# A gated state-space and retention block on one core: left operands of two matrix products split straight from SBUF, half of the squares folded by VectorE, S5's constants computed in pieces

## The chip, the cores and the metric

The kernel runs on one core of a Trainium2 chip (trn2). The metric is the device time of one execution in microseconds (us), and the figure for a kernel is the median of its runs. TensorE does the matrix products, ScalarE and VectorE prepare their operands and take the results, GpSimd and SyncE mostly issue transfers.

## The reference

Input x is 1024 tokens by 2048 channels in float32. One layer is computed:

```
h = RMSNorm_pre(x);  P = h @ W_in      # columns: u, s5 gate, q, k, v, ret gate, two merge gates
y_s = S5(u) -> GELU -> half-GLU, times SiLU(s5 gate)
y_r = retention(q, k, v) -> per-head RMSNorm, times SiLU(ret gate)
m = sigmoid(g_s) * (y_s @ W_s) + sigmoid(g_r) * (y_r @ W_r)
x = x + RMSNorm_post(m @ W_out)
```

S5 is a diagonal complex recurrence. Its constants come from `lam_re`, `lam_im` and `log_step` (64 groups by 64 states): `step = exp(log_step)`, `mag = exp(lr * step)`, the cosine and sine of `li * step`, their powers up to the eighth, and a factor that scales B.

## The kernel before

**Matrix products.** All of them are cut into 16 output groups, in this order: u, v, zr, zs, gs0, gs1, qk, glu, gr0, gr1, ws0, ws1, wr0, wr1, out0, out1 (`GU`, `GV`, ... `GO1`). Each group is a 2 by 2 block product by a Strassen-Winograd scheme with seven products, p = A11, S1, S2, S4, S3, A12, A22 in order of time, and each product is 8 steps (4 in glu and ws0 to wr1), one for each tile of 128 in the inner dimension. That makes 756 steps. `at` is the number of a step in its group, 0 to 55. S1 = A21 + A22, S2 = S1 - A11, S4 = A12 - S2, S3 = A11 - A21 are sums of blocks of the left operand; the right operand's sums are made by `weights_summed`, one tile ahead by three steps.

**One step.** The products have nearly float32 precision: both 128x512 operands are split into a rounded part and the rest. ScalarE makes `a_hi` and `b_hi` (`heads`, L643 and L653), VectorE makes `a_lo` and `b_lo` (`rests`, L1085 and L1087), and TensorE does 12 matmuls of 512 columns (`multiply`, L1469 to L1475): four output tiles by hi*hi, hi*lo, lo*hi. The four rings have `RING = 3` slots, so that ScalarE can start step s only when step s-3 is done. Every engine has one program, a loop over the steps, and works in its written order: on VectorE a step is `weights_summed(s + 3)`, `rests(s)`, then evacuations (`evacuate`, 128x2048) and whatever else has been given to this step.

**Left operands.** They go through HBM. The blocks and their sums are written to `aops` (`store_ops`, 1 MB in each of two transfers) and read back a tile of 256 KB at a time into the 4 slots of `araw` (`load_a`, SyncE's queue). This holds for h in group u and for m in group out0 too, which stand whole in SBUF (`h_t`, `m_t`) while their first group runs. There each product's stores stand in SyncE's queue just ahead of its first load, which waits for them: at u's step 0 A11, at 8 S1, and so on; in out0 A12, A22 and S3 are stored at step 12. The sums are made by `left_sums`: in u and out0, at steps 5 and 6 S1, 7 and 8 S3 (in place over A21), 11 and 12 S2, 18 and 19 S4, each a 128x2048 operation. S2 overwrites S1's buffer, and S4 that of S2, so each waits for the store of the one before.

**Start.** x comes transposed in eight transfers of 1 MB (`load_x`) on SyncE's queue, four of them ahead of the first weights. ScalarE squares each (128x2048, L629), TensorE adds over partitions with a matrix of ones (L1437, four float32 matmuls for each, which the profile records as eight), ScalarE takes the root (L633, L635), VectorE the reciprocal (L1048) and scales h (`scale_h`, L1052, 128x512). The squares have a ring of two. VectorE first computes two exponentials (`magnitudes`). It scales half 0 of the tokens (16 operations) ahead of step 0, half 1 at steps 1 to 4, four each.

**S5's constants.** In group v VectorE computes `angles` (step 2), `quadrants` (4), `powers` (6) and `factors` (8), all chains of 128x64 operations each of which waits for the last; then `inputs_scaled` (9 to 16, 128x1024) and 24 `window_part`s (20 to 43), and in zr 24 `m3_part`s (4 to 27), one in a step. TensorE takes the windows after v's last step and the scan's inputs after zr's. In out0 and out1 `take_rows` scales results into `o_row`, which lies over `m_t`; `merge` (wr1 and the first steps of out0) completes m.

**ScalarE as a queue.** ScalarE also issues the stores of the results: u's go out in 16 transfers with short rows (L727), four at steps 37, 45 and 53 of u and 5 of v.

Of the kernel before, what the change touches and what calls it, by code (L numbers as in the profile page):

```python
# [90 lines left out]

def sums_before(g, p, k):

    order = {1: 0, 2: 1, 4: 2, 6: 3}
    return 4 * sum(TILES[:g]) + order[p] * TILES[g] + k
# [7 lines left out]
def build_program(nc, x, xT, wstream, gain_in, gain_out, b_glu, lam_re, lam_im, log_step,  # L103
                  b_ri, b_ir, c_ri, c_ir, d_rep, signs, eye, ones, dmat, zeta, xi,
                  gdec, rope, aops, spill, vrows, turned, m1d, m2d, m3d, out):
    with ExitStack() as ctx:
# [51 lines left out]
        powers_tmp = area(14336, 1024).rearrange("p (n g) -> p n g", n=16)  # L158
# [48 lines left out]
        rstd = keep[:, 2, 0:1024].rearrange("p (i n) -> p i n", i=2)  # L207
# [4 lines left out]
        squared, sums_done = sem("squared"), sem("sums_done")  # L212
# [60 lines left out]
        def token_as_step(a):  # L273
            return a.rearrange("p n (c t) -> p n t c", t=STEP)

# [34 lines left out]
        def _(sp):  # L310
# [31 lines left out]
            def store_ops(g, p):  # L342

                last = g == GO0
                for n in range(2):
                    ks = slice(4 * n, 4 * n + 4)
                    src = h_t if not last else m_t
                    if p in (A11, A12, A22):
                        i, first = (1, 8) if p == A22 else (0, 8 if p == A12 else 0)
                        if not last:  # L350
                            sp.wait_ge(h_ready, 16 * i + first + 4 * n + 4)
                        else:
                            sp.wait_ge(gated, {A11: 11, A12: 15, A22: 16}[p])
                        sp.dma_start(op_block(OP_BASE[g] + 8 * p + 4 * n), src[:, i, first + 4 * n:first + 4 * n + 4, :]
                                     ).then_inc(op_stored[p], 16)
                    else:
                        order = {S1: 0, S3: 1, S2: 2, S4: 3}[p]
                        sp.wait_ge(s_ready, (8 if last else 0) + 2 * order + n + 1)
                        if p == S3:
                            src = src[:, 1, ks, :]  # L360
                        elif last:
                            src = s_out(n).rearrange("p (k m) -> p k m", k=4)
                        else:
                            src = s_buf[:, ks, :]
                        sp.dma_start(op_block(OP_BASE[g] + 8 * p + 4 * n), src).then_inc(op_stored[p], 16)

            def load_a(s):
# [4 lines left out]
                if g in (GU, GO0):  # L372
                    sp.wait_ge(op_stored[p], 64 if g == GO0 else 32)
# [60 lines left out]
            for k in range(4):  # L434
                load_b11(0, k)
            for q in range(4, 8):
                load_x(q)
            for k in range(4, 8):
                load_b11(0, k)
            for s in range(STEPS):  # L440
                g, p, k = place(s)
                at = s - BASE[g]
                if g == GU and k == 0:
                    store_ops(g, p)
                if g == GO0 and k == 0 and p < 4:
                    store_ops(g, p)
                if g == GO0 and at == 12:
                    for later in (A12, A22, S3):
                        store_ops(g, later)
                load_a(s)  # L450
                if s >= A_RING:
# [3 lines left out]
                    if p4 == 6 and g4 + 1 < len(TILES):  # L455
                        load_b11(g4 + 1, k4)
# [79 lines left out]
                if g == GO0 and at == 36:  # L536
                    for p2 in (S1, S2, S4):
                        sp.wait_ge(op_stored[p2], 64)
                    sp.dma_start(gain_row, gain_out).then_inc(gain_row_loaded, 16)
# [17 lines left out]
        def _(pool):  # L557
# [4 lines left out]
            for p in range(7):  # L562
                pool.wait_ge(op_stored[p], 32)
            for dst, src in ((bb_p, b_ri), (bb_q, b_ir), (cc_p, c_ri), (cc_q, c_ir)):
                pool.dma_start(dst.rearrange("p g h -> p (g h)"), src).then_inc(params_loaded, 16)
# [52 lines left out]
        def _(act):  # L618
# [4 lines left out]
            act.wait_ge(eps_ready, 1)  # L623
            for q in range(8):
# [6 lines left out]
                if q == 4:  # L631
                    act.wait_ge(sums_done, 4)
                    A.activation(rstd[:, 0, :], psum[:, 4, :], ACT.Sqrt, scale=1.0 / D_MODEL, bias=eps_sb[:, 0:1]).then_inc(std_ready, 1)  # L633
            act.wait_ge(sums_done, 8)
            A.activation(rstd[:, 1, :], psum[:, 5, :], ACT.Sqrt, scale=1.0 / D_MODEL, bias=eps_sb[:, 0:1]).then_inc(std_ready, 1)  # L635

            def heads(s):
                g, p, k = place(s)
                r = s % RING
                act.wait_ge(a_loaded[s % A_RING], 16 * (s // A_RING + 1))  # L640
# [14 lines left out]
            def free(b, g):  # L655

                if g == 0:
                    act.wait_ge(sums_done, 8)
                    act.wait_ge(h_ready, 32)
# [157 lines left out]
            for s in range(STEPS + TAIL):  # L817
                if s < STEPS:
                    heads(s)
                over = ended(s - 3)  # L820
# [30 lines left out]
        def _(dve):  # L851
# [41 lines left out]
            def magnitudes():  # L893
                dve.wait_ge(rates_loaded, 5 * 16)
                exp(s0, step_sb, s1, s2, s3)
# [4 lines left out]
            def angles():  # L900
# [8 lines left out]
                then(V.scalar_tensor_tensor(s1, s3, -4.0, s1, ALU.mult, ALU.add))  # L909
                tt(s5, s2, s2, ALU.mult)  # L910
                poly(s6, s5, [2.7557319e-6, -1.98412698e-4, 8.33333333e-3, -1.66666667e-1, 1.0])
                tt(s6, s6, s2, ALU.mult)
                poly(s7, s5, [2.48015873e-5, -1.38888889e-3, 4.16666667e-2, -0.5, 1.0])

            def quadrants():
# [9 lines left out]
                tt(s7, s7, s6, ALU.add)  # L925
                ts(s3, s1, 2.0, ALU.is_ge, -2.0, ALU.mult)
# [8 lines left out]
            def powers():  # L935
# [4 lines left out]
                for m in (1, 2, 4):  # L940
                    re_m = pow_re[:, m:m + 1, :].broadcast_to([P, m, GROUPS])
                    im_m = pow_im[:, m:m + 1, :].broadcast_to([P, m, GROUPS])
                    p_rr, p_ii, p_ri, p_ir = [powers_tmp[:, 4 * n:4 * n + m, :] for n in range(4)]
                    V.tensor_tensor(p_rr, pow_re[:, 1:1 + m, :], re_m, ALU.mult).then_inc(setup_step, 1)
                    V.tensor_tensor(p_ii, pow_im[:, 1:1 + m, :], im_m, ALU.mult).then_inc(setup_step, 1)
                    V.tensor_tensor(p_ri, pow_re[:, 1:1 + m, :], im_m, ALU.mult).then_inc(setup_step, 1)
                    V.tensor_tensor(p_ir, pow_im[:, 1:1 + m, :], re_m, ALU.mult).then_inc(setup_step, 1)
                    steps[0] += 4
                    dve.wait_ge(setup_step, steps[0])
                    V.tensor_tensor(pow_re[:, m + 1:2 * m + 1, :], p_rr, p_ii, ALU.subtract).then_inc(setup_step, 1)  # L950
                    steps[0] += 1
                    tt(pow_im[:, m + 1:2 * m + 1, :], p_ri, p_ir, ALU.add)

            def factors():
# [3 lines left out]
                then(V.reciprocal(s1, s1))  # L958
# [8 lines left out]
                tt(par_im, s2, s1, ALU.mult)  # L967
                for par in range(2):
# [74 lines left out]
            magnitudes()  # L1043
            dve.wait_ge(consts_loaded, 5 * 16)

# [8 lines left out]

            invert(0)
            for k in range(16):
# [23 lines left out]
            def rests(s):  # L1080
# [4 lines left out]
                V.tensor_tensor(a_lo[:, r, :], araw[:, s % A_RING, :], a_hi[:, r, :].bitcast(F32), ALU.subtract).then_inc(split, 1)  # L1085
# [11 lines left out]
            def left_sums(g, a, at):  # L1097

                last = g == GO0
                for n in range(2):  # L1100
                    ks = slice(4 * n, 4 * n + 4)
                    k2 = slice(8 + 4 * n, 12 + 4 * n)
                    s_n = s_out(n).rearrange("p (k m) -> p k m", k=4) if last else s_buf[:, ks, :]
                    done = 8 if last else 0
                    stores = 64 if last else 32
                    if at == 5 + n:
                        if last:
                            dve.wait_ge(gated, 16)
                        else:
                            dve.wait_ge(h_ready, 32)  # L1110
                        V.tensor_tensor(s_n, a[:, 1, ks, :], a[:, 1, k2, :], ALU.add).then_inc(s_ready, 1)
                    if at == 7 + n:
                        dve.wait_ge(s_ready, done + n + 1)
                        V.tensor_tensor(a[:, 1, ks, :], a[:, 0, ks, :], a[:, 1, ks, :], ALU.subtract).then_inc(s_ready, 1)
                    if at == 11 + n:
                        dve.wait_ge(op_stored[S1], stores)
                        V.tensor_tensor(s_n, s_n, a[:, 0, ks, :], ALU.subtract).then_inc(s_ready, 1)
                    if at == 18 + n:
                        dve.wait_ge(op_stored[S2], stores)
                        V.tensor_tensor(s_n, a[:, 0, k2, :], s_n, ALU.subtract).then_inc(s_ready, 1)  # L1120
# [163 lines left out]
            def take_rows(g, p):  # L1284
# [7 lines left out]
                if g == GO0 and p == 3:  # L1292
                    dve.wait_ge(gain_row_loaded, 16)
                    for op in range(7):
# [414 lines left out]
```

## Time and profile before

| | us |
|---|---|
| median of 3 runs | 2518.59 |
| lowest and highest | 2516.74, 2531.87 |
| profiled execution: time | 2524.69 |
| profiled execution: span | 2522.9 |

The profile is of one execution. Its span is 1.8 us shorter than its time; the execution is 6.1 us above the median. Busy shares in it are averages over stages with different limits, so that the steps of the prediction go by stretches of time.

### The profile page before, as it was taken

What the parts mean: (1) busy time and instruction counts of PE and PEld (TensorE: products, weight loads), DVE (VectorE), ACT (ScalarE), POOL (GpSimd) and SP (SyncE); (2) the same over time, 40 slices, a digit from 0 to 9 for tenths busy, and PEclk for the clock granted to TensorE, in tenths of its full rate; (3) what the DMA queues carried; (4) which work ended last, traced back from release to release, by engine and by line L of the source; (5) the groups of instructions that cost most, each with busy time, mean ns of one, the idle gap of its engine ahead of it and who ended that gap; (6) DMA issues with size and microseconds to landing.
All of it is one profiled execution on the core that took longest, in us unless ns stands there. A gap on an engine that the chain in (4) does not pass through costs nothing.

```text
span 2522.9 us, 28579 instructions
## 1 busy us (share of the span) xinstructions
PE 2332.7 (92%) x10288; PEld 1892.8 (75%) x10288; DVE 1853.4 (73%) x2968; ACT 1150.8 (46%) x1814; POOL 85.2 (3%) x99
## 2 busy tenths in 40 slices
PE   7898999998999999988989996989999999799994
PEld 3676778787888888886777774767887777578883
DVE  6857992977898886626887754777678988767676
ACT  4343443456555554553445443334555444245552
POOL 0000000000000000000000000440000000000000
PEclk9999997999999999999999997899999999999997
DMA  7678456765456473769555767255656655855546
GB/s 271 217 232 253 133 171 217 262 209 197 120 183 211 145 244 111 256 199 296 180 184 157 280 187 255 68 201 175 212 196 210 224 185 180 291 200 189 182 130 254
DMA packets 287888, 508.67 MB, mean 202 GB/s; under 512 B 53201, under 2 KB 69601, under 8 KB 285569
## 3 DMA queue, kind: packets, MB, share of 16 engines
q1 hardware_dynamic: 242672, 430.00, 52.1%
q10 hardware_dynamic: 36560, 46.27, 5.3%
q0 software_dynamic: 8512, 30.56, 3.7%
q8 instruction: 81, 1.33, 0.2%
q14 instruction: 63, 0.51, 0.1%
HBM read 394.54 MB, written 112.20 MB: 201 GB/s over the span
## 4 chain that ended last, share of the span: by engine, by line
PE 67%; DVE 16%; DMA 6%; issue 4%; ACT 3%; SPq 3%; ACTq 1%; POOL 0%; DVEq 0%; POOLq 0%
PE psum L1473 16%; PE psum L1474 16%; PE psum L1475 16%; PE psum L1469 4%; PE psum L1471 4%; PE psum L1470 4%; DMA araw<-aops 4%; DVE a_lo L1085 3%; DVE b_lo L1087 3%; PE psum L1580 1%; PE psum L1578 1%; ACT a_hi L643 1%; DVE keep L1095 1%; PE psum L1529 1%; DMA aops<-work 1%
## 5 line engine op out<-in xcount | busy, mean ns | idle before, releaser
L643 ACT ACTIVATE a_hi<-araw 128x512 fp32r<-128x512 f32 x756 | 476.5, 630 | 1197.5 <-PE psum L1475 760.8
L1473 PE MATMUL psum<-a_hi,b_hi 128*128 128x512 f32 x2352 | 930.9, 396 | 97.8 <-DVE b_lo L1087 90.7
L1474 PE MATMUL psum<-a_hi,b_lo 128*128 128x512 f32 x2352 | 923.7, 393 | 0.0
L1475 PE MATMUL psum<-a_lo,b_hi 128*128 128x512 f32 x2352 | 922.8, 392 | 0.0
L1085 DVE TENSOR_TENSOR a_lo<-araw,a_hi 128x512 fp32r<-128x512 f32 x756 | 520.9, 689 | 535.5 <-ACT a_hi L643 534.1
L1473 PEld LDWEIGHTS psum<-a_hi,b_hi 128*128 128x128 f32 x2352 | 446.6, 190 | 213.5 <-DVE b_lo L1087 107.7
L1475 PEld LDWEIGHTS psum<-a_lo,b_hi 128*128 128x128 f32 x2352 | 446.5, 190 | 94.5
L1474 PEld LDWEIGHTS psum<-a_hi,b_lo 128*128 128x128 f32 x2352 | 446.8, 190 | 91.6
L1469 PE MATMUL psum<-b_hi,a_hi 128*128 128x512 f32 x672 | 268.4, 399 | 30.2 <-DVE b_lo L1087 29.6
L1087 DVE TENSOR_TENSOR b_lo<-bx,b_hi 128x512 fp32r<-128x512 f32 x432 | 295.5, 684 | 0.0
L653 ACT ACTIVATE b_hi<-bx 128x512 fp32r<-128x512 f32 x432 | 266.5, 617 | 0.5 <-DMA bx<-in_wstream 0.2
L1470 PE MATMUL psum<-b_lo,a_hi 128*128 128x512 f32 x672 | 265.6, 395 | 0.0
L1471 PE MATMUL psum<-b_hi,a_lo 128*128 128x512 f32 x672 | 265.1, 394 | 0.0
L1469 PEld LDWEIGHTS psum<-b_hi,a_hi 128*128 128x128 f32 x672 | 128.5, 191 | 66.6 <-DVE b_lo L1087 34.8
L1471 PEld LDWEIGHTS psum<-b_hi,a_lo 128*128 128x128 f32 x672 | 128.6, 191 | 27.4
L1470 PEld LDWEIGHTS psum<-b_lo,a_hi 128*128 128x128 f32 x672 | 128.7, 191 | 26.4
L1087 DVE TENSOR_TENSOR b_lo<-bz,b_hi 128x512 fp32r<-128x512 f32 x216 | 147.8, 684 | 0.0
L653 ACT ACTIVATE b_hi<-bz 128x512 fp32r<-128x512 f32 x216 | 133.2, 617 | 0.0
L692 ACT ACTIVATE keep<-psum 128x2048 f32<-128x2048 f32 x63 | 117.4, 1863 | 7.0 <-PE psum L1471 6.9
L1095 DVE TENSOR_TENSOR keep<-psum,keep 128x2048 f32<-128x2048 f32 x48 | 109.6, 2283 | 0.0
L1067 DVE TENSOR_TENSOR bx<-by,bx 128x512 f32<-128x512 f32 x108 | 74.1, 686 | 2.0
L1071 DVE TENSOR_TENSOR bx<-bz,bx 128x512 f32<-128x512 f32 x108 | 73.9, 684 | 1.8
(147 smaller groups left out, 1618.8 us busy)
## 6 DMA issues: line engine op xcount, KB each, us to landing
araw<-aops SPq DMA_DIRECT2D x744, 256.0 KB, 2.7
bz<-in_wstream SPq DMA_DIRECT2D x216, 256.0 KB, 3.7
bx<-in_wstream SPq DMA_DIRECT2D x116, 256.0 KB, 4.7
aops<-work SPq DMA_DIRECT2D x28, 1024.0 KB, 5.7
spill<-keep ACTq DMA_DIRECT2D x28, 1024.0 KB, 5.8
by<-in_wstream SPq DMA_DIRECT2D x108, 256.0 KB, 5.5
work<-spill SPq DMA_DIRECT2D x20, 1024.0 KB, 7.6
aops<-work POOLq DMA_DIRECT2D x15, 1024.0 KB, 5.4
```

The lines of the kernel that those rows point to most:

```text
L643: A.activation(a_hi[:, r, :], araw[:, s % A_RING, :], ACT.Copy).then_inc(head, 1)
L653: A.activation(b_hi[:, r, :], src[:, k, :], ACT.Copy).then_inc(head, 1)
L692: A.activation(kept_view(g, b), bank_view(g, banks), func).then_inc(act_evac, 1)
L1085: V.tensor_tensor(a_lo[:, r, :], araw[:, s % A_RING, :], a_hi[:, r, :].bitcast(F32), ALU.subtract).then_inc(split, 1)
L1087: V.tensor_tensor(b_lo[:, r, :], src[:, k, :], b_hi[:, r, :].bitcast(F32), ALU.subtract).then_inc(split, 1)
L1095: V.tensor_tensor(kept_view(g, b), bank_view(g, banks), kept_view(g, b), ALU.add).then_inc(dve_evac, 1)
L1469: T.matmul(bank, a_hi[:, r, cols], b_hi[:, r, :], start=first, stop=False, skip_group_check=on)
L1470: T.matmul(bank, a_hi[:, r, cols], b_lo[:, r, :], start=False, stop=False, skip_group_check=on)
L1471: done = T.matmul(bank, a_lo[:, r, cols], b_hi[:, r, :], start=False, stop=last, skip_group_check=on)
L1473: T.matmul(bank, b_hi[:, r, cols], a_hi[:, r, :], start=first, stop=False, skip_group_check=on)
L1474: T.matmul(bank, b_lo[:, r, cols], a_hi[:, r, :], start=False, stop=False, skip_group_check=on)
L1475: done = T.matmul(bank, b_hi[:, r, cols], a_lo[:, r, :], start=False, stop=last, skip_group_check=on)
```

## The change

- **Left operands in u and out0.** The new function `left(s)` gives the tile of `h_t`, `s_buf`, `m_t` or `s_out`, and `heads` and `rests` read it there. `load_a` isn't called in these groups. ScalarE waits for VectorE's semaphores (`h_ready`, `s_ready`, `gated`) in place of a load's. The stores of the blocks stay, for the later groups, at steps 16 (S1), 18 (A11), 20 (A22), 24 (S2), 32 (S4), 36 (A12), 40 (S3) of SyncE's program. The first group that reads them back is v, or out1.
- **Sums.** In u they are made a tile at a time (`sum_h`, 128x512): S1 at steps 4 to 11, together with the scaling of the two tiles of half 1 that it needs, S2 at 14 to 21, S4 at 22 to 29 together with the scaling of A12's tile, S3 at 30 to 37. Ahead of step 0 stand only 8 of the 16 scalings. The second reciprocal stands at step 3. In out0 (`sum_m`, 128x2048): S1 at 5 and 6, S2 at 14 and 18, S4 at 22 and 26, S3 at 28 and 30.
- **Squares.** For half 0 VectorE adds the four tiles of each square (`fold`), and TensorE does one matmul in place of four. Half 1 stays with TensorE; its last two squares are summed between steps 0 and 1 and between 1 and 2. x and the first weights are loaded alternately. A root of one column ahead of the squares loads ScalarE's table.
- **Constants.** One exponential stays at the start, ahead of the folds. The rest goes to u's steps 38 (`magnitudes`), 42, 44, 46, 48, 50, 52, 54 and v's 0, 2, 4, 6. `inputs_scaled` moves to 8 to 15, `window_part` to two of three steps in 17 to 52, `m3_part` in zr to two of three steps in 4 to 39.
- **Rows out.** out0's four `take_rows` move to out1's steps 1 to 4.

```
+            if p == A11:
+                return whole[:, 0, k, :]
...
             for s in range(STEPS):
...
+                if g in (GU, GO0):
+                    if at == 16:
+                        store_ops(g, S1)
...
+                else:
+                    load_a(s)
...
-                A.activation(a_hi[:, r, :], araw[:, s % A_RING, :], ACT.Copy).then_inc(head, 1)
+                A.activation(a_hi[:, r, :], left(s), ACT.Copy).then_inc(head, 1)
...
+            def fold(q):
+
+                dve.wait_ge(squared, q + 1)
+                V.tensor_tensor(sq_ring[:, q % 2, 0:1024], sq_ring[:, q % 2, 0:1024], sq_ring[:, q % 2, 1024:2048], ALU.add
+                                ).then_inc(folded, 1)
+                dve.wait_ge(folded, 2 * q + 1)
+                V.tensor_tensor(sq_ring[:, q % 2, 0:512], sq_ring[:, q % 2, 0:512], sq_ring[:, q % 2, 512:1024], ALU.add
+                                ).then_inc(folded, 1)
...
             invert(0)
-            for k in range(16):
+            for k in range(8):
                 scale_h(0, k)
...
+            def sum_h(p, k):
+
+                a11, a12, a21, a22 = h_t[:, 0, k, :], h_t[:, 0, 8 + k, :], h_t[:, 1, k, :], h_t[:, 1, 8 + k, :]
+                if p == S1:
+                    dve.wait_ge(h_ready, h_order(1, 8 + k) + 1)
+                    V.tensor_tensor(s_buf[:, k, :], a21, a22, ALU.add).then_inc(s_ready, 1)
+                elif p == S2:
+                    dve.wait_ge(s_kept[k // 4], 16)
+                    V.tensor_tensor(s_buf[:, k, :], s_buf[:, k, :], a11, ALU.subtract).then_inc(s_ready, 1)
...
                 if g == GU:
+                    if at == 3:
+                        invert(1)
+                    if 4 <= at < 12:
+                        scale_h(1, at - 4)
+                        scale_h(1, at + 4)
+                        sum_h(S1, at - 4)
+                    if 14 <= at < 22:
+                        sum_h(S2, at - 14)
+                    if 22 <= at < 30:
+                        scale_h(0, at - 14)
+                        sum_h(S4, at - 22)
+                    if 30 <= at < 38:
+                        sum_h(S3, at - 30)
+                    if at == 38:
+                        magnitudes()
+                    if at == 42:
+                        quarter_turns()
...
+                if s in (0, 1):
+                    sum_squares(6 + s)
```

## Rows read from the trace of the kernel before

**Rows 1.** The profile's page: busy time by engine

```profile
PE 2332.7 (92%) x10288; PEld 1892.8 (75%) x10288; DVE 1853.4 (73%) x2968; ACT 1150.8 (46%) x1814; POOL 85.2 (3%) x99
```

**Rows 2.** Busy time by stretch: length, then each engine's (instructions), granted clock, DMA

```profile
45.65:95.40 49.75, 39.66 (x144) 30.15 (x145) 46.56 (x56) 16.14 (x27) 0.00 (x0) 0.89 0.60 206
95.40:221.85 126.45, 122.07 (x530) 100.05 (x529) 81.85 (x119) 53.67 (x90) 2.12 (x4) 0.99 0.76 248
221.85:390.15 168.30, 157.38 (x661) 124.57 (x660) 152.47 (x267) 70.17 (x114) 4.79 (x7) 0.98 0.56 171
426.70:587.00 160.30, 155.92 (x661) 126.42 (x662) 121.42 (x169) 73.61 (x115) 9.92 (x16) 0.97 0.73 239
764.20:916.50 152.30, 152.30 (x674) 126.11 (x673) 132.60 (x372) 77.71 (x120) 0.00 (x0) 1.00 0.56 180
2154.45:2239.90 85.45, 66.17 (x254) 51.89 (x253) 60.91 (x71) 29.28 (x45) 0.00 (x0) 0.88 0.78 283
```

**Rows 3.** The chain of waits, 0 to 82 us: start, length, what

```profile
9.93 16.96 PE psum L1437 x32
27.74 3.36 DVE keep L1048
31.13 5.40 DVE work L1052 x8
36.55 4.42 DMA aops<-work
40.98 2.66 DMA araw<-aops
...
54.07 2.66 DVE work L1052 x4
```

**Rows 4.** The timeline, 0 to 28 us: start, length, engine, what, idle before

```profile
15.21 0.34 PEld L1437 LDWEIGHTS psum<-keep,ones_sb 128*128 128x128 f32 x1 [0.52 <-issue]
...
16.41 0.19 PEld L1437 LDWEIGHTS psum<-keep,ones_sb 128*128 128x128 f32 x1 [0.24 <-issue]
16.42 0.48 DVE L867 TENSOR_TENSOR work<-work 128x64 f32<-128x64 f32 x2
16.67 1.91 ACT L629 ACTIVATE keep<-work 128x2048 f32<-128x2048 f32 x1 [4.56 <-PE psum L1437]
...
22.22 0.48 DVE L867 TENSOR_TENSOR work<-work 128x64 f32<-128x64 f32 x2
```

**Rows 5.** VectorE's timeline in u: a right and a left operand's sum

```profile
64.35 0.69 DVE L1067 TENSOR_TENSOR bx<-by,bx 128x512 f32<-128x512 f32 x1
...
66.16 2.28 DVE L1111 TENSOR_TENSOR work<-work 128x2048 f32<-128x2048 f32 x1
```

**Rows 6.** ScalarE's timeline in u: its issues of u's stores

```profile
160.47 6.67 ACTq L727 DMA_DIRECT2D turned<-keep  x2
...
186.81 5.59 ACTq L727 DMA_DIRECT2D turned<-keep  x2
...
209.59 3.16 ACTq L727 DMA_DIRECT2D turned<-keep  x2
```

**Rows 7.** VectorE's timeline in v: first and last of `angles`, one of `inputs_scaled`

```profile
223.98 0.65 DVE L862 TENSOR_SCALAR work<-work 128x64 f32<-128x64 f32 x3
...
230.33 0.20 DVE L862 TENSOR_SCALAR work<-work 128x64 f32<-128x64 f32 x1
...
260.87 1.22 DVE L867 TENSOR_TENSOR work<-work 128x1024 f32<-128x1024 f32 x1
```

**Rows 8.** ScalarE's timeline in out0: the a_hi with the longest waits ahead

```profile
2187.22 0.63 ACT L643 ACTIVATE a_hi<-araw 128x512 fp32r<-128x512 f32 x1 [15.36 <-DMA araw<-aops]
...
2209.80 0.63 ACT L643 ACTIVATE a_hi<-araw 128x512 fp32r<-128x512 f32 x1 [14.64 <-DMA araw<-aops]
```

**Rows 9.** VectorE's timeline at out0's start: the merges that complete m

```profile
2151.90 2.28 DVE L1279 TENSOR_TENSOR work<-work,keep 128x2048 f32<-128x2048 f32 x1
...
2154.22 2.29 DVE L1282 TENSOR_TENSOR work<-work 128x2048 f32<-128x2048 f32 x1
```

More of the change, by code:

```diff
@@ L274, in token_as_step, with left @@
             return a.rearrange("p n (c t) -> p n t c", t=STEP)
+        def left(s):
+            g, p, k = place(s)
+            if g not in (GU, GO0):
+                return araw[:, s % A_RING, :]
+            whole = m_t if g == GO0 else h_t
+            if p == A11:
+                return whole[:, 0, k, :]
+            if p == A12:
+                return whole[:, 0, 8 + k, :]
+            if p == A22:
+                return whole[:, 1, 8 + k, :]
+            if p == S3:
+                return whole[:, 1, k, :]
+            return s_out(k // 4)[:, COLS * (k % 4):COLS * (k % 4) + COLS] if g == GO0 else s_buf[:, k, :]
         def main_banks(g):
@@ L442, in _ @@
                 at = s - BASE[g]
[L443 to L450, printed above, removed]
+                if g in (GU, GO0):
+                    if at == 16:
+                        store_ops(g, S1)
+                    if at == 18:
+                        store_ops(g, A11)
+                    if at == 20:
+                        store_ops(g, A22)
+                    if at == 24:
+                        store_ops(g, S2)
+                    if at == 32:
+                        store_ops(g, S4)
+                    if at == 36:
+                        store_ops(g, A12)
+                    if at == 40:
+                        store_ops(g, S3)
+                else:
+                    load_a(s)
                 if s >= A_RING:
@@ L560, in _ @@
                 pool.dma_start(dst, src).then_inc(consts_loaded, 16)
-            for p in range(7):
+            for p in (A11, S4, S3, A12, A22):
                 pool.wait_ge(op_stored[p], 32)
+            pool.wait_ge(split, 2 * BASE[GV])
             for dst, src in ((bb_p, b_ri), (bb_q, b_ir), (cc_p, c_ri), (cc_q, c_ir)):
@@ L621, in _, with square @@
                 act.dma_start(dst, src).then_inc(rates_loaded, 16)
-            act.wait_ge(eps_ready, 1)
-            for q in range(8):
+            def square(q):
                 act.wait_ge(x_loaded[q], 16)
@@ L630, in _, with root @@
                              ).then_inc(squared, 1)
[L631 to L635, printed above, removed]
+            def root(i):
+                act.wait_ge(sums_done, 4 * i + 4)
+                A.activation(rstd[:, i, :], psum[:, 4 + i, :], ACT.Sqrt, scale=1.0 / D_MODEL, bias=eps_sb[:, 0:1]).then_inc(std_ready, 1)
+            act.wait_ge(eps_ready, 1)
+            A.activation(rstd[:, 1, 0:1], eps_sb[:, 0:1], ACT.Sqrt)
+            for q in range(4):
+                square(q)
+            root(0)
+            square(4)
+            square(5)
             def heads(s):
@@ L819, in _ @@
                     heads(s)
+                if s == 0:
+                    square(6)
+                if s == 1:
+                    square(7)
+                if s == 2:
+                    root(1)
                 over = ended(s - 3)
@@ L957, in factors @@
                 tt(s1, s1, s2, ALU.add)
-                then(V.reciprocal(s1, s1))
+                V.reciprocal(s1, s1).then_inc(powers_ready, 1)
+                dve.wait_ge(powers_ready, 1)
+            def factors():
                 ts(s0, pow_re[:, 1, :], -1.0, ALU.add)
@@ L967, in factors, with scan_factors @@
                 tt(par_im, s2, s1, ALU.mult)
+            def scan_factors():
                 for par in range(2):
@@ L1053, in scale_h @@
                                        ALU.mult, ALU.mult).then_inc(h_ready, 1)
+            for q in range(4):
+                fold(q)
             invert(0)
-            for k in range(16):
+            for k in range(8):
                 scale_h(0, k)
@@ L1084, in rests @@
                 dve.wait_ge(head, 2 * s + 1)
-                V.tensor_tensor(a_lo[:, r, :], araw[:, s % A_RING, :], a_hi[:, r, :].bitcast(F32), ALU.subtract).then_inc(split, 1)
+                V.tensor_tensor(a_lo[:, r, :], left(s), a_hi[:, r, :].bitcast(F32), ALU.subtract).then_inc(split, 1)
                 dve.wait_ge(head, 2 * s + 2)
@@ L1293, in take_rows @@
                     dve.wait_ge(gain_row_loaded, 16)
-                    for op in range(7):
+                    for op in (A11, S4, S3, A12, A22):
                         dve.wait_ge(op_stored[op], 64)
@@ L1368, in _ @@
+                if g == GV:
+                    if at == 0:
+                        more_powers(4)
                     if at == 2:
-                        angles()
+                        inverse_rates()
                     if at == 4:
-                        quadrants()
+                        factors()
                     if at == 6:
-                        for op in range(7):
-                            dve.wait_ge(op_stored[op], 32)
-                        powers()
-                    if at == 8:
-                        factors()
```

248 lines of the change are left out of this document (149 added, 99 removed).

## The prediction

> **What bounds the kernel now.** The page comes first: TensorE is busy 92% of the span [rows 1]. That number doesn't say what a change at an edge is worth, so the second view is busy time by stretch, cut at starts of steps. The undisturbed middle sets the unit: group gs0 takes 152.3 us for 56 steps [rows 2], 2.72 us a step, with TensorE never idle. Each other stretch is held against that. u's steps 0 to 11 take 49.75 us for 12 x 2.72 = 32.6, so 17.1 are lost; u's other 44 steps lose 126.45 - 119.7 = 6.8; v's first 55 lose 168.3 - 149.6 = 18.7; zr's first 55 lose 10.7; out0's first 21 lose 85.45 - 57.1 = 28.3. Ahead of all that lies the start, 45.7 us until the first step. The third view, the chain of waits [rows 3], shows what the start is made of: sums on TensorE, a reciprocal, eight scalings, then 4.4 us for a store to land and 2.7 us for a load of the same data. The fourth, the timelines of ScalarE and VectorE, tells whose the losses are: in out0 ScalarE sits idle 15.4 and 14.6 us until a load of `araw` [rows 8], in v VectorE works on its small operations for 6.5 us at a stretch [rows 7]. A step needs some 1.2 us of splitting on VectorE (four scalings of 2.66 us with it made a period of 3.85 in u [rows 3]) and 0.6 for a right operand's sum, if several follow closely. So it has about 0.9 us a step to give away.
>
> The slack matters below. ScalarE may split step s when s-3 is done, and the halves are ready some 1.9 us after that (a_hi, b_hi, then b_lo), 3.5 us ahead of need. One delay of up to 3.5 us on VectorE costs nothing.
>
> **The start, to step 12.** Removed: the store and load in front of step 0 (4.42 + 2.66) [rows 3]. Added: the folds, behind one exponential. That exponential ends at 16.66, halfway in the first row of the pair [rows 4]; TensorE began its sums at 9.93 [rows 3], so the folds start later than the sums did. A fold is a 128x1024 and a 128x512 operation, 1.22 [rows 7] and 0.69 [rows 5], with a wait 1.95. Its matmul is two of the eight records of a square; they stood 0.86 apart (0.34 + 0.52) until about 16 us and 0.43 apart (0.19 + 0.24) after it [rows 4], so the one now takes about 1.7 at the lower of the clock's two levels (1.2 GHz). With a ring of two the third square (1.91) waits for the first sum: 16.7 + 1.95 + 1.7 = 20.4, square to 22.4, the fourth to 24.4, fold to 26.4, sum to 28.1, root 28.9, reciprocal (3.36) to 32.4, eight scalings (5.4) to 37.8, first split to 39.1. The sums of half 0 end 1.2 us later than the 26.89 of before; nothing is gained there. TensorE meanwhile has squares 4 and 5 to sum, 16 records from 30.9: seven at the lower level (6.0) and nine at 0.43, to 40.8. It is the later of the two, so step 0 starts at 40.8, not 45.7. The two moved sums (8 x 0.43 = 3.4 each) then lie on TensorE between steps 0 to 2: 53.1. ScalarE's root of half 1 waits for them, `heads(3)` is queued behind it, VectorE splits step 3 by 55.8, and its reciprocal (3.36) holds up the split of step 4, which TensorE starts at 60.5. Steps 4 to 11 each add two scalings and a sum, 2 x 0.67 + 0.65, to 0.6 and 1.2: 3.8 us a step, bound by VectorE. Step 12 starts at 60.5 + 30.4 = 90.9, against 95.4: **4.5 us gained**. The bounds: all of the 16 records at the lower level (13.7) take 3.9 off; none there adds 1.7, as the splits are ready at 39.1. So 0.6 to 6.2.
>
> Here the trace speaks first on a second point: a 128x2048 sum took 2.28, a 128x512 one 0.69 [rows 5]. The Trainium skill, "VectorE: DVE Perf Modes", section on the TRN2 errata, says that SBUF-source operations pay a fixed latency for each instruction, so that many small tiles pay it each, and this speaks against sums by tiles. The rows agree: 4 x 0.69 is 0.48 more than 2.28, in 8 replaced operations 3.8 us of VectorE's time. Operations that follow each other closely start 0.60 apart, which would leave 1.6.
>
> **u from step 12.** S2's sums make a step 0.6 + 0.6 + 1.2 = 2.4, S4's with a scaling 2.5, S3's 2.4: under 2.72, nothing lost, but hardly any slack is rebuilt. ScalarE waits for these sums two steps ahead of need. S2 and S4 overwrite what is being stored, but the stores of 1 MB have at least three steps (8 us) for the 4.4 of [rows 3]; SyncE's queue has no loads waiting behind them up to step 36, where loads of weights come that have four steps to spare. Lost before were 6.8, nearly all where ScalarE was held by the issue of u's stores: the second pairs of issues took 6.7 and 5.6 us at steps 37 and 45, against 3.2 at 53, which cost nothing [rows 6]. These stay. With less traffic about (56 loads are gone) they may shrink; I take no gain. New is the chain of small operations: `magnitudes` 6.0 (16.66 to 22.70 in [rows 4]), the former `angles` 6.5 for 27 operations [rows 7], 0.24 each, so 4.4 for the 18 of the quadrants and some 3.4 for those of the powers. In steps 38 to 55 VectorE gets 18 x 1.2 + 8 x 0.6 + two evacuations of 2.2 + 20.3 = 51.1 us for 49.0 of TensorE. That is 2.1 over. And `magnitudes` comes right after the issue at step 37, when all slack is used: 6.0 + 1.2 against 2.72 loses up to 4.5. Between 0 (the issues shrink and slack absorbs it) and 9 (both, with the lower clock behind the gap) I take **5 lost**.
>
> **v and zr.** Gone from v's first 16 steps are 20 us of small operations, what is left (powers of m = 4, the reciprocal, `factors`, the copies) is about 7.5 in 8 steps: 8 x 1.2 + 3 x 0.6 + 7.5 = 18.9 under 21.8. `inputs_scaled` makes 0.6 + 1.2 + 1.22 = 3.05 a step, 0.33 over, 2.6 in eight steps, within the slack. The window parts at two in three steps average 0.8 and fit. Of 18.7 lost I leave 1.7 (a late load at step 21 and an evacuation): **17 gained**, 13 to 18. ScalarE's evacuation of u's last product now waits for VectorE at v's step 2, with 1.3 us to spare. In zr the m3 parts' excess goes: **1.5 gained**, 0 to 2; the other 9 lie with a low clock after the windows and a late load at step 20, which stay.
>
> **out0 and out1.** No step waits for a store or a load of m now. What is late next is VectorE: two merges of 4.5 [rows 9] at steps 0 and 4 and two sums of 2.2 at 5 and 6. Run by hand from step 0 at 2154.5: step 1 0.7 late, steps 5, 6 and 7 0.2, 1.4 and 1.4 late, and from then on sums 4 steps apart fit. **28.3 becomes 3.2, 25 gained**, 20 to 27. The weights' loads are no longer queued behind A11's store. In out1 four `take_rows` of 2.2 follow each other with 1.2 each: 0.7 over a step, 2.8, within the slack; **0.5 lost**, 0 to 3.
>
> **The sum.** 4.5 - 5 + 17 + 1.5 + 25 - 0.5 = 42.5. The profiled execution's 2524.7 becomes 2482.2. It lies 6.1 above the median of the runs; from the median, 2518.6 - 42.5 = 2476.1. All terms at their lower ends give 0.6 - 9 + 13 + 0 + 20 - 3 = 21.6, 2497; at the upper 6.2 + 0 + 18 + 2 + 27 - 0 = 53.2, 2465.
>
> **Rivals.** (1) The queue of ScalarE lets go: with u's loads away the issues at 37 and 45 take 4 us like the later ones and cost nothing, and u from 12 gains 4.7 (6.8 less the 2.1 over) where I have 5 lost. Against it, S3's store stands at the same place as A12's did. Net 52, 2467. Start 0.6, u 9 lost, the rest as forecast: net 34.6, with v's at its low end 30.6, 2488. (3) A store takes the loads' place in out0: SyncE's stores of S1 wait behind A22's and the weights', and VectorE, which waits for S1's landing at step 14, holds all splits. Before, such landings cost 14.6 us of ScalarE's time [rows 8]. Then out0 gains 10: net 27, 2491. (4) Slower than before: ScalarE waits for VectorE's sum, VectorE for ScalarE's a_hi, both in written order. From the rows the round (split 1.2, right sum 0.6, left sum 0.6, a_hi and b_hi 1.2, waits 0.2) is 3.8 us for a lead of two steps, 5.44. It decides from 5.44 on; to eat 42.5 us over the 32 steps of u and the 24 of out0 that use sums, it would have to be 5.44 + 2 x 0.76, 7 us, and to be slower by 1% (25 us) 7.9. Nothing in the trace is near it.
>
> **Chances.** Forecast 0.62, (1) 0.13, (2) 0.12, (3) 0.09, (4) 0.04. The range that leaves out (4) and the tails goes from 2462 to 2500. A change of under 1% (25 us) a measurement of this kernel hardly tells from none; the line is 2493.4. The forecast's own low end and the worse halves of (2) and (3) cross it: faster 0.86, within 1% 0.10, slower 0.04.
>
> **What would show it.** The first multiply at about 41, two groups of float32 sums between it and step 2, step 12 at 91; no ScalarE wait on `araw` in u or out0; VectorE the releaser in steps 4 to 11 and at 38, 39 and 48 to 52 of u; v's first 55 steps in 151 us, out0's first 21 in 60; gs0 at 152.3 as before. I am wrong if a wait on a store shows on VectorE, if u's steps 12 to 55 take over 135 us, or if TensorE's matmuls stand 0.43 apart in steps 4 to 11.

## The result, and the profile after

The changed kernel takes 2483.06 us (median of 4 runs, 2476.33 to 2490.07), the kernel before 2519.27 us in the same comparison. The ratio is 0.9847, with a 95% interval of 0.9803 to 0.9891: 36 us less (27 to 50 by that interval), where 42.5 were forecast; the time forecast, 2476.1, was 7.0 too low and the measured one lies inside the range of 2462 to 2500. The profiled execution took 2480.14 us, with a span of 2478.3.

Busy time by stretch in the changed kernel, cut at the starts of the same steps as [rows 2] (length, then each engine's busy time and instructions, granted clock, DMA share, GB/s):

```profile
40.25:91.30 51.05, 42.86 (x162) 29.37 (x160) 38.78 (x58) 18.80 (x30) 0.00 (x0) 1.00 0.11 40
91.30:224.20 132.90, 125.52 (x529) 101.85 (x530) 116.64 (x241) 53.12 (x89) 2.12 (x4) 0.96 0.54 175
224.20:377.80 153.60, 151.95 (x662) 123.15 (x660) 138.00 (x201) 69.83 (x114) 4.79 (x7) 1.00 0.63 192
415.50:570.70 155.20, 153.07 (x661) 126.11 (x662) 121.12 (x169) 73.63 (x115) 9.92 (x16) 0.98 0.74 248
752.00:904.30 152.30, 152.30 (x673) 126.13 (x672) 132.70 (x373) 77.72 (x120) 0.00 (x0) 1.00 0.56 180
2134.10:2195.10 61.00, 58.38 (x254) 47.03 (x253) 52.79 (x68) 29.29 (x45) 0.00 (x0) 1.00 0.59 217
```

Group gs0, the fifth row, takes 152.3 us again, so 2.72 us stays the unit. Against it the other rows give the terms of the prediction:

| stretch | lost before | lost after | gained | forecast |
|---|---|---|---|---|
| start of step 12 | 95.4 | 91.3 | 4.1 | 4.5 |
| u, steps 12 to 55 | 6.8 | 13.2 | -6.4 | -5 |
| v, 55 steps | 18.7 | 4.0 | 14.7 | 17 |
| zr, 55 steps | 10.7 | 5.6 | 5.1 | 1.5 |
| out0, 21 steps | 28.3 | 3.9 | 24.4 | 25 |
| out1 | 0 | 0.3 | -0.3 | -0.5 |
| sum | | | 41.6 | 42.5 |

The two spans differ by 44.6, 3.0 more than the table: one stretch that the change doesn't touch, the retention, is 7.9 shorter, and the other untouched stretches are 5.0 longer together; the last section says more of this. The medians differ by 36.2. The profiled execution of the kernel before was 5.4 above its median and that of the changed kernel 2.9 below its own.

The start, in the chain of waits of the changed kernel (start, length, what), answers to [rows 3]:

```profile
16.52 1.24 DVE keep L1136
17.78 0.70 DVE keep L1139
18.62 2.06 PE psum L1575 x2
20.77 1.92 ACT keep L676
22.71 1.24 DVE keep L1136
...
29.28 1.91 ACT keep L676
31.23 9.61 PE psum L1579 x16
43.59 3.44 PE psum L1579 x8
49.80 3.45 PE psum L1579 x8
...
55.73 3.36 DVE keep L1144
```

The folds (L1136, L1139) and their single matmuls are on the chain, squares 4 and 5 take TensorE 9.6 us, the last two sums 3.4 each between steps, and the second reciprocal ends at 59.1. No store or load of h is left in it.

What ScalarE waited for behind u's step 36 and at the start of v, from its timeline (start, length, what, idle before):

```profile
156.55 4.82 ACTq L795 DMA_DIRECT2D turned<-keep  x2
161.48 0.63 ACT L708 ACTIVATE a_hi<-work 128x512 fp32r<-128x512 f32 x1 [6.02 <-issue]
...
227.74 1.88 ACT L760 ACTIVATE keep<-psum 128x2048 f32<-128x2048 f32 x1 [2.16 <-DVE work L1039]
```

The first row is the issue of u's stores again, 4.8 us where it had been 6.7 [rows 6]; the second is the split that it held back. The last is the evacuation that waits for VectorE's reciprocal at v's step 2.

### The profile page after: what moved, and what is told of

Its sections match the earlier page's. It is cut to its first block, busy times and chain, and to the rows that moved or that the text cites. A ratio compares the mean times of both kernels' runs of the same rounds, so it can differ in the third digit from the quotient of the medians.

```text
span 2478.3 us, 28348 instructions
## 1 busy us (share of the span) xinstructions
PE 2306.3 (93%) x10264; PEld 1877.6 (76%) x10264; DVE 1861.2 (75%) x3000; ACT 1149.0 (46%) x1814; POOL 85.8 (3%) x99
## 4 chain that ended last, share of the span: by engine, by line
PE 72%; DVE 15%; issue 4%; DMA 4%; ACT 3%; SPq 2%; ACTq 1%; DVEq 0%; POOL 0%
PE psum L1619 17%; PE psum L1620 16%; PE psum L1621 16%; PE psum L1615 5%; PE psum L1617 5%; PE psum L1616 5%; DVE a_lo L1183 3%; DVE b_lo L1185 3%; DMA araw<-aops 2%; PE psum L1726 1%; PE psum L1724 1%; PE psum L1675 1%; DVE bx L1165 1%; ACT a_hi L708 1%; ACT work L837 1%
## 5 line engine op out<-in xcount | busy, mean ns | idle before, releaser
L708 ACT ACTIVATE a_hi<-araw 128x512 fp32r<-128x512 f32 x644 | 405.9, 630 | 974.1 <-PE psum L1621 703.2
L1183 DVE TENSOR_TENSOR a_lo<-araw,a_hi 128x512 fp32r<-128x512 f32 x644 | 443.7, 689 | 432.5 <-ACT a_hi L708 431.5
L1615 PE MATMUL psum<-b_hi,a_hi 128*128 128x512 f32 x672 | 263.0, 391 | 4.3 <-DVE b_lo L1185 4.1
L708 ACT ACTIVATE a_hi<-work 128x512 fp32r<-128x512 f32 x112 | 70.6, 630 | 176.5 <-PE psum L1621 97.0
L1183 DVE TENSOR_TENSOR a_lo<-work,a_hi 128x512 fp32r<-128x512 f32 x112 | 77.0, 688 | 55.3 <-ACT a_hi L708 54.8
```

Of the source, the lines that this page charges most:

```text
L708: A.activation(a_hi[:, r, :], left(s), ACT.Copy).then_inc(head, 1)
L1183: V.tensor_tensor(a_lo[:, r, :], left(s), a_hi[:, r, :].bitcast(F32), ALU.subtract).then_inc(split, 1)
L1615: T.matmul(bank, a_hi[:, r, cols], b_hi[:, r, :], start=first, stop=False, skip_group_check=on)
```

## The experiments

All differences from the kernel before are from the ratios measured with each run. The stretches come from each kernel's own profile. From e2 on, every kernel is an edit of the changed one. A step's loss is the time from its start to the next step's, less 2.72 us, so that a late step shows as a loss of the one before. The edits are shown shortened, some lines joined.

**e1: out0's part alone.** On the kernel before, out0's left operands come straight from m, with its sums, stores and `take_rows` as in the change. It also leaves out eight needless loads of `bx` at the ends of groups qk and gr1, as the changed kernel does (116 such loads before, 108 after).

```
-                load_a(s)
+                if g == GO0:
+                    if at in when: store_ops(g, when[at])
+                else:
+                    load_a(s)
-                A.activation(a_hi[:, r, :], araw[:, s % A_RING, :], ACT.Copy)
+                A.activation(a_hi[:, r, :], left(s), ACT.Copy)
```

> The kernel before with out0's part of the change alone: left operands of out0 straight from m, its sums and stores and take_rows as in the changed kernel; u, v, zr and the start as before. Theory: out0 lost its time to the store and reload, so out0's first 21 steps go from 28.3 us over 21 x 2.72 to about 4, and the whole time falls by 23 to 26 us. Rival: less traffic is what helped, or the executions differ by chance (the retention ahead of gr1 took 7.9 us less in the changed kernel's profile); then out0's share of the gain is under 15 us and the stretches elsewhere move too.

2491.78 us, ratio 0.9901 (0.9866 to 0.9936). Out0's first 21 steps:

```profile
2148.30:2209.20 60.90, 58.27 (x253) 46.97 (x252) 52.69 (x68) 29.29 (x45) 0.00 (x0) 1.00 0.58 213
```

60.9 us, 3.8 lost for the 28.3 of before, and 25 to 26 us less in all (0.0099 x 2518; 16 to 34 by the interval). The start, u, v and the losses in them stayed within 0.5 us of the kernel before. One stretch elsewhere did move, as the rival said: the retention was again 8 us shorter. But out0's own stretch gives 24.5 us, so its gain stands by itself. It is the largest term, 24.4 of the 41.6 in the table.

**e2: the pieces of the constants back in v.** `inputs_scaled` also goes back to steps 9 to 16.

```
-                    if at == 42: quarter_turns()   ... 54: more_powers(2)
+ (v)                if at == 2:  quarter_turns(); sines(); cosines()
+                    if at == 4:  swap_quadrants(); sign_quadrants()
+                    if at == 6:  first_powers(); more_powers(1); (2); (4)
+                    if at == 8:  inverse_rates(); factors(); scan_factors()
```

> The changed kernel with S5's constants, from the quarter turns on, back in v's steps 2, 4, 6 and 8 in one piece each and inputs_scaled at 9 to 16; magnitudes stays at u's step 38, windows stay spread. Theory: u's steps 44 to 55 lose some 4 us less and v's first 16 steps 11 to 12 more (2.5 to 14), net 8 us slower than the changed kernel. Rival: VectorE has the same work in both groups, so the pieces only move the loss; then u and v together stay within 3 us.

2494.55 us, ratio 0.9904 (0.9873 to 0.9934), 11 us over the changed kernel's median. Steps 36 to 55 of u and 0 to 15 of v, first in this kernel, then in the changed one:

```profile
156.90:220.40 63.50, 57.21 (x241) 46.49 (x240) 40.45 (x77) 22.85 (x40) 2.12 (x4) 0.95 0.54 158
220.40:278.10 57.70, 48.42 (x193) 36.26 (x193) 53.65 (x138) 21.77 (x35) 0.00 (x0) 0.97 0.55 179
```

```profile
156.80:224.20 67.40, 60.03 (x242) 47.66 (x241) 54.15 (x144) 22.84 (x40) 2.12 (x4) 0.92 0.53 153
224.20:270.20 46.00, 45.50 (x194) 35.34 (x192) 40.19 (x74) 21.66 (x34) 1.63 (x2) 1.00 0.70 221
```

VectorE's busy time is the same in both, 94.1 and 94.3 us. In one piece it costs 121.2 us, spread 113.4. The 7.8 between them is what the pieces are worth in these two stretches, against 8 expected. The rival, that pieces only move the loss, is out. (The whole times alone don't show it: the intervals of the two ratios overlap.)

**e3: no folds.** VectorE's `fold` is left out and TensorE sums four tiles of each square of half 0.

> The changed kernel without the folds: TensorE sums all four tiles of each square of half 0 again. Theory (the prediction's chain): the folds sit behind the exponential and gain nothing; the sums of half 0 end at 26.9 in place of 28.7, the reciprocal starts at 27.7 in place of 29.4, TensorE is already at its upper clock level for squares 4 and 5 and ends them at about 35, so step 0 starts at 37.8, 2.5 us earlier than in the changed kernel, and step 12 at 88.8. Rival: TensorE's longer sums are the bound, as the folds were meant to relieve it; then the first step starts later than 40.3.

2475.28 us, ratio 0.9825 (0.9809 to 0.9842). TensorE's timeline at the start:

```profile
9.46 16.03 PE L1573 MATMUL psum<-keep,ones_sb 128*128 128x512 f32 x32 [9.46 <-DMA gdec_sb<-in_gdec]
28.07 7.13 PE L1573 MATMUL psum<-keep,ones_sb 128*128 128x512 f32 x16 [2.58 <-ACT keep L676]
36.40 0.50 PE L1613 MATMUL psum<-a_hi,b_hi 128*128 128x512 f32 x1 [1.19 <-DVE b_lo L1183]
```

Squares 4 and 5 take 7.1 us in place of 9.6 and step 0 starts at 36.4, 3.9 ahead of the changed kernel (2.5 expected), and step 12 at 87.1 (88.8 expected). It is then VectorE's split that TensorE waits for. The folds cost time in both ways that the prediction named. They wait for the exponential. And TensorE, which in e3 had been busy for 16.0 us when it came to squares 4 and 5, had done 7.0 us of work in three separate pieces in the changed kernel; its granted clock over these squares was 1.00 in e3 and 0.72 there.

**e4: `magnitudes` at u's step 40.** One number changed: `if at == 38` to `if at == 40`.

> The changed kernel with magnitudes at u's step 40 in place of 38, two steps behind ScalarE's issue of u's stores. Theory: what is lost at 38 and 39 (4.5 + 2.6 us) is lost because the 6.0 us on VectorE come when its lead of two steps has just been used up by the issue; with the lead restored some 1 to 2 us remain, and u's steps 36 to 55 lose 13.0 - 5 = 8 us. Rival: it is the sum of VectorE's work from 38 to 55 (51 us for 49) that costs, whatever its place; then the loss only moves to 41 and 42 and stays over 11.

2478.82 us, ratio 0.9839 (0.9822 to 0.9855). u's steps 36 to 55:

```profile
156.90:218.70 61.80, 55.83 (x241) 44.63 (x240) 53.91 (x144) 22.84 (x40) 2.11 (x4) 1.00 0.55 160
```

VectorE is as busy as before (53.9 and 54.2 us), but 20 steps take 61.8 us, not 67.4; the loss is 7.4 in place of 13.0, and the granted clock of the stretch is 1.00, not 0.92. Of the 5.6, 4.0 lie in steps 38 to 47, where `magnitudes` stands. The other 1.6 lie at steps 51 and 52, where nothing was edited. The chain of waits of the changed kernel shows the place:

```profile
156.55 3.19 ACTq L795
...
161.48 0.64 ACT a_hi L708
...
169.41 0.69 DVE a_lo L1183
170.10 0.61 DVE b_lo L1185
170.75 0.80 PE psum L1619
171.55 0.43 PE psum L1620
```

After ScalarE's issue the lead is gone, `magnitudes` fills the time to 169.4, TensorE stands idle for over 4 us and then begins step 39 with matmuls 0.43 apart, at 1.2 GHz. Steps 38 and 39 of the changed kernel, as stretches:

```profile
163.49:170.75 7.26, 3.04 (x12) 2.17 (x13) 6.40 (x28) 2.37 (x5) 0.00 (x0) 0.91 0.54 156
170.75:176.04 5.29, 5.29 (x13) 4.13 (x13) 2.35 (x4) 0.00 (x0) 0.00 (x0) 0.50 0.17 50
```

So 4.5 us are lost by the wait, and 2.6 by the step behind it, in which TensorE never stops but has half the clock. The same happens, less surely, behind the late step 50: it loses 2.1 in every kernel whose quadrants stand there, and step 51 then has a granted clock of 0.69 in the changed kernel, 0.62 in e6 and 1.00 in e4, e7 and e8. That is the 1.6. The loss at 38 is one of place. The remaining sum of work, the rival, costs 7.4 at most.

**e5: window and m3 parts in every step.**

```
-                    if 17 <= at < 53 and (at - 17) % 3 < 2: window_part(...)
+                    if 20 <= at < 44:  window_part(at - 20)
-                    if 4 <= at < 40 and (at - 4) % 3 < 2:   m3_part(...)
+                    if 4 <= at < 28:   m3_part(at - 4)
```

> The changed kernel with the window parts in v and the m3 parts in zr back at one in every step, as in the kernel before (steps 20 to 43 and 4 to 27). Theory: three quarters of the gain in v's steps 16 to 54 and zr's steps 0 to 54 (4.6 + 10.6 before, 1.5 + 5.5 after) comes from spreading these parts, for a part of 1.22 us on top of 1.2 and 0.6 goes 0.3 us over a step; the loads that come late at zr's step 20 then find VectorE with no lead. So these two stretches lose 13 to 15 us. Rival: the late load itself, which differs from execution to execution, made the difference; then they stay at 7.

2480.37 us (2 runs), ratio 0.9854 (0.9826 to 0.9883). v's steps 16 to 54 take 110.8 us where the changed kernel takes 107.6, the 3.2 that spreading is worth there. zr's first 20 steps lose 4.4 against 1.5 (the spread kernels lose 1.5 to 2.9 there, e1 4.1). Its steps 20 to 54 lose 6.4 against 4.0, but the kernels e6 to e9, whose parts are spread, lose 5.0 to 7.3 there. So some 2 of zr's 5.1 belong to the change; the rest differs from execution to execution: 1.0 at step 0, which lost 2.5 in the kernel before and in e3, e4 and e9, 1.5 in the changed one, and 2.4 behind the late load at step 20. Expected were 13 to 15 us in these stretches, measured 15.5. The number was met, but the other kernels with spread parts lose 6.6 to 10.3 in the two stretches together, so that the rival, the late load, holds for a part of it. This run's whole time can't tell: its profile has a much faster stretch elsewhere, see the last section.

**e6: no folds, `magnitudes` at the start.**

> No folds, and magnitudes at the start behind the first exponential, where VectorE waits for the sums of squares anyway. Theory: the start stays at 36.4 (VectorE has 10 us free ahead of the reciprocal at 27.7) and u's steps 36 to 55 lose 6 in place of 13, which is 11 us less than the changed kernel in all: 2472 by the median of 2483. Rival: step 38 costs because ScalarE's issue is long; then u's steps 36 to 55 still lose over 9.

2473.93 us, ratio 0.9824 (0.9805 to 0.9843). u's steps 36 to 55:

```profile
152.50:212.00 59.50, 57.22 (x241) 45.87 (x240) 49.03 (x119) 22.85 (x40) 2.12 (x4) 0.97 0.60 174
```

5.1 lost. Step 0 starts at 36.3, so the second exponential costs nothing where VectorE waits for sums. These stretches show 12.1 us against the changed kernel, 4.2 up to step 12 and 7.9 here. The medians show 9.1 and the two spans 8.2, among other things because zr lost 2.8 more in this execution.

**e7: all sums of squares ahead of step 0.**

```
-            for q in range(6):
+            for q in range(8):
                 sum_squares(q)
...
-                if s in (0, 1):
-                    sum_squares(6 + s)
```

> As the one before, and all eight sums of squares stand ahead of step 0 in TensorE's program. TensorE's work is the same, but ScalarE's second root, with step 3's splits queued behind it, no longer waits for sums between the steps. Theory: step 0 starts at 43.3, 7 later, but step 4 at 54.5 (56.3 without folds) and step 12 at 84 to 85 (87.1). Rival: step 12 is set by VectorE's 3.8 us a step from step 4 on and step 4 by step 0; then step 12 comes later than 87.

2462.04 us, ratio 0.9774 (0.9756 to 0.9792). Steps 0 to 11, and 36 to 55 of u:

```profile
41.00:81.90 40.90, 35.09 (x146) 26.55 (x144) 36.49 (x54) 15.89 (x26) 0.00 (x0) 1.00 0.12 43
147.30:205.20 57.90, 55.64 (x241) 44.74 (x240) 48.98 (x119) 22.87 (x40) 2.13 (x4) 1.00 0.59 169
```

Step 0 starts later than in e6, at 41.0 against 36.3, but step 4 3.9 us earlier, at 52.3 against 56.2, and step 12 5.2 earlier, at 81.9 against 87.1. All three come 2 to 3 us earlier than expected, for the forecast put step 0 later by the two sums in full. TensorE has the same work. In e6 steps 0 to 3 lose 9.0 us, 6.7 at steps 0 and 1, which have the sums behind them, and 2.3 at steps 2 and 3; here they lose 0.4. So of the 3.9 at step 4 some 2 are the wait in ScalarE's written order that is gone, a root that waits for sums and holds back step 3's splits. Another 1.2 is time in which TensorE stood idle ahead of step 0 in e6, waiting for a split, and now sums, and 0.4 is an earlier start of the sums in this execution. The other 1.3 by step 12 come mostly at step 4, which loses nothing here and 1.1 in e6. In u's steps 36 to 55 the loss is 3.5 for e6's 5.1; the difference is step 51, at a granted clock of 1.00 here and 0.62 in e6, where both have the same program. The medians of e6 and e7 differ by 11.9 us; the stretches named here account for 6.8 of them.

**e8: the second reciprocal and the scalings a step earlier.** On e7, `invert(1)` at step 2, the scalings and S1's sums at 3 to 10.

> As the one before, and VectorE's second reciprocal stands at step 2 and the scaling of half 1 with S1's sums at steps 3 to 10, a step earlier. Theory: VectorE's lead over TensorE is filled in the first three steps, so step 12 starts at 79 to 81, and the whole time is 18 to 20 us under the changed kernel's. Rival: the reciprocal now waits for the root while the split of step 3 is due and nothing is gained over the one before.

2462.57 us, ratio 0.9787 (0.9772 to 0.9802), no different from e7. Steps 0 to 11 take 39.2 us, 1.7 less, and step 0 started 0.6 later in this execution, so step 12 is at 80.8. The gain is there in the stretch but too small for the medians.

**e9: the pieces moved once more.** On e7, quarter turns to cosines at u's 39 to 41, quadrants at 44 and 46, powers at 48, 49, 52 and 54, the reciprocal at 53, `inputs_scaled` at two of three steps from v's 5.

> The kernel with all sums of squares ahead of step 0, no folds and magnitudes at the start, and the pieces of S5's constants moved off the places where they still cost: quarter turns to cosines to u's steps 39 to 41, the quadrants to 44 and 46 (away from the evacuation at 50), the powers to 48 to 54, the reciprocal to 53, so that ScalarE's evacuation at v's step 2 finds its buffer free; inputs_scaled at two of three steps from v's 5. Theory: each loss left there (2.2 at u's step 50, 0.7 at v's step 6, 0.35 a step at v's 10 to 15) is a place where VectorE has more than its lead, so u's steps 36 to 55 lose 1 in place of 3.5 and v's first 16 under 1 in place of 3: 4 to 5 us less, 2457 to 2458. Rival: VectorE's work from u's step 39 to v's step 16 is as much as TensorE's, so what leaves one place is lost at another, and the two stretches stay at 6 to 7.

2463.65 us over 5 runs, ratio 0.9774 (0.9752 to 0.9795). u's steps 36 to 55 and v's 0 to 15:

```profile
150.30:206.20 55.90, 55.31 (x242) 44.71 (x241) 50.82 (x130) 22.97 (x40) 2.12 (x4) 1.00 0.60 173
206.20:251.00 44.80, 44.05 (x193) 35.84 (x192) 39.10 (x64) 21.53 (x34) 2.52 (x4) 1.00 0.74 243
```

1.5 and 1.3 lost, where e7 lost 3.5 and 3.0: the theory holds for the stretches, by 3.7 us, at u's step 50 (0.4 for 2.1) and at `inputs_scaled`, which lost nothing. v's steps 5 to 7 lost 1.4, not less than before (1.2 in e7), though ScalarE's evacuation at v's step 2 no longer waited. The whole isn't faster than e7, nor could 4 us be told from none here; the profiled execution started step 0 3.0 us later and lost 6.8 more in the retention. The best kernels are e7, e8 and e9, which can't be told apart, some 20 us under the changed kernel and 2.1 to 2.3% under the one before.

## Why the prediction was right

The mechanism held: each term's time was lost or gained at the places and by the waits that it named. That the table's sum is 41.6 for 42.5 is in part luck: u and v together fell 3.7 short of the forecast, and zr gave 3.6 more than forecast, most of which the change didn't make. Without that surplus the terms give 38.

**What bounds the kernel.** The reading by stretches held: the stretches that the change doesn't touch kept their length within 2.5 us but for one, the retention, 7.9 us shorter (last section), and the gain lies where the losses were.

**Start.** Step 0 at 40.3 (forecast 40.8), step 4 at 60.5 (60.5), step 12 at 91.3 (90.9). The chain was right in each piece, the lower clock for squares 4 and 5 among them (9.9 us forecast, 9.6 measured). e3 shows that "nothing is gained there" was too mild: the folds cost 3.9 us. e7 shows the second cost that the sum contained but didn't name as one, the two sums between the steps and the root behind them: 3.9 us at step 4 and 5.2 at step 12.

**u from step 12.** -6.4 for -5, by the two places that were named: 7.1 at steps 38 and 39, behind ScalarE's issue, and 4.3 at steps 48 to 52, with the evacuation. Of these, 2.6 and 1.6 are steps at a lower granted clock (0.50 at step 39). e4 and e6 confirm the first, e9 the second. Rival 1, shorter issues, was half true: they fell from 6.7, 5.6 and 3.2 to 4.8, 1.9 and 1.9 us, step 37 lost 1.3 in place of 2.9 and step 45 nothing in place of 1.8; but this was not enough to give `magnitudes` room. In e3 step 37 lost only 0.1, and step 38 still 4.5.

**v.** 14.7 for 17. The mis-sized term is "within the slack". `inputs_scaled` lost 0.31 to 0.35 a step in steps 10 to 14, 1.9 us with its ends. The slack had been spent before. ScalarE's evacuation waited 2.2 us for VectorE at v's step 2, where the prediction gave it 1.3 us to spare, and ScalarE's last issue of u's stores held it 4.4 us just ahead of its splits for step 6; steps 6 and 7 lost 0.6. Which of the two spent the lead isn't shown: in e9 the evacuation's wait is gone, and steps 5 to 7 lose 1.4. That `inputs_scaled` has no room at one in every step is shown: at two of three it lost nothing in e9. e2 is the direct proof of the rest, and e5 for the window parts.

**zr.** 5.1 for 1.5. The term itself was right: steps 1 to 19, where the m3 parts' excess lay, lost 1.7 in the kernel before and nothing in the changed one. The other 3.4, at step 0 and from the late load at step 20 on, differ between executions: the kernels with spread parts lost 5.6 to 9.4 in zr, the three with a part in every step 10.6 to 11.3.

**out0 and out1.** 24.4 for 25, with the late steps that were forecast: steps 5 and 6 lost 1.3 each, so that steps 6 and 7 began late, for 1.4 each forecast. e1 shows that nothing but this edit is needed. Rival 3, a wait on a store, had no row: VectorE waited for nothing but ScalarE's a_hi in out0's first 21 steps.

**Small tiles.** What the Trainium skill, "VectorE: DVE Perf Modes", section on the TRN2 errata, says of many small tiles was on the side of the trace and cost little: steps 4 to 11, with sums of 128x512, stood 3.86 us apart, forecast 3.8.

**Rival 2**, u and the start at the lower clock: the granted clock was 1.00 in steps 0 to 11, and 0.96 in the rest of u, where the lower level showed behind late steps alone.

**Rival 4** did not come about: steps 12 to 35 of u, with sums two steps ahead, lost 0.2 us.

## What to carry to other kernels

Where two engines work in written order with a lead of a few steps, price an edit by the lead at its place and not by busy shares: 6 us of VectorE's work cost 7 us behind ScalarE's long issue (2.6 of them a step at the lower clock), 3 two steps later, and nothing at the start. An operand that already stands in SBUF should not go round through HBM for its first use; the store can follow at leisure. Moving work off an engine early in a kernel can cost more than it saves, when its replacement waits for something else and the engine then does its next work at the lower clock.

## What the runs showed of the hardware

TensorE's granted clock fell in two stretches in which it was busy nearly all the time, with short float32 operations, and not in the same way in every execution. (It fell behind waits too: 0.50 in u's step 39, after 4 us of standing idle.) The windows are 128x128 transposes and matmuls of 16 columns, the retention mostly matmuls of 128 columns. The first 20 us of the windows behind v, in the changed kernel and in e5, with the same program there:

```profile
380.30:400.30 20.00, 18.69 (x117) 18.50 (x116) 1.29 (x2) 8.07 (x12) 0.00 (x0) 0.60 0.52 202
```

```profile
382.30:402.30 20.00, 18.69 (x194) 18.50 (x192) 1.29 (x2) 11.65 (x18) 0.00 (x0) 1.00 0.64 239
```

Busy 18.7 us in both, 117 instructions at a granted clock of 0.60 and 194 at 1.00. The stretch lost 35.0 us in the one and 21.3 in the other; the other profiles had 33 to 35. And 20 us of the retention ahead of gr1, in the kernel before and in the changed one:

```profile
1568.90:1588.90 20.00, 18.98 (x87) 14.47 (x88) 4.68 (x10) 4.43 (x6) 0.00 (x0) 0.50 0.00 0
```

```profile
1554.20:1574.20 20.00, 18.97 (x116) 13.99 (x116) 10.52 (x14) 6.42 (x9) 1.10 (x1) 0.91 0.00 1
```

This stretch lost 101.8 us in the kernel before, in e3 (101.8) and in e9 (100.7), and 93.8 or 93.9 in the eight others, whatever the edit. It is 7.9 us of the 44.6 between the two profiled spans and goes with no edit. Runs of one kernel spread over 6 to 21 us; the two stretches, with 8 and 14 us between their levels, are of that size, though no run shows that they make all of it. What decides which level an execution gets stays open; no experiment was made on it.
